# The opening of a fused transformer block: who splits and sums the input tiles, which queue loads the first two weight units, and who splits the memory units

## The chip, the cores and the metric

The kernel runs on one core of a Trainium2 chip. The metric is the device time of one execution in microseconds (us); a kernel's number is the median of its runs. The engines are TensorE (PE in the profile; PEld is its weight load), VectorE (DVE), ScalarE (ACT), GpSimd (POOL), and SyncE (SP), which issues most of the DMAs. ACT can issue DMAs too, on a queue of its own.

## The reference, cut to what matters

Two transformer blocks follow each other on 1024 tokens of width 1024, all in fp32. What the change touches is the head of the first:

```python
def rms_norm(x, w):
    y = x * lax.rsqrt(jnp.mean(x * x, axis=-1, keepdims=True) + 1e-6)
    return y * w

h = rms_norm(x, norm_w)                      # x: 1024 tokens x 1024
proj = einsum('bsd,de->bse', h, w_in)        # 1024 -> 6160: gq, gk, gv, glr, hq, ...
m = rms_norm(mem, mem_norm_w)                # mem: 256 tokens x 1024
mkv = einsum('bmd,de->bme', m, w_mem_kv)     # 1024 -> 1024: mk, mv
# two gated linear attentions, one cross attention over mk and mv, gate, w_out,
# then a convolution block and an MLP of width 4096 (the second block)
```

## The kernel before, in words

Activations lie transposed: x is eight tiles `xr[k]` (in RES) of 128 features by 1024 tokens. Weights come in "units" of 128 x 1024 fp32 (512 KB), listed in `UNITS` in the order of their use: unit 0 is `glr`, 1 `gq` of head 0, 2 `gk`, 3 and 4 `gv` of head 0, 5 to 8 the memory keys `mk`, 9 to 12 the memory values `mv`, 13 `gq` of head 1, and so on. There are four slots, so unit q is loaded when unit q - 4 has been read.

TensorE multiplies in a rounded fp32 form, so each operand is split into a high part (a rounded copy) and a low part (the rest), and a product is three matmuls: high weight with high data, high weight with low data, low weight with high data. A weight unit's high part goes to WH and its low part to WL. The low part is always a subtraction on GpSimd (L2480); the high part is a copy by ScalarE (through the helper at L1647) or by GpSimd (L2478), as the plan's `hi_by` says: ScalarE for units 0 and 1, GpSimd for those after them. Data goes to HB in the same way: the high part of an x tile (times `norm_w`) by ScalarE for even k and by GpSimd for odd k (L2463), the low part by VectorE (`stt` at L1963).

The norm's sum of squares: ScalarE squares each tile (L1666), and the squares are added into two accumulators, the even tiles on VectorE (`tt`, L1960), the odd ones on GpSimd (L2470). `x_sum` (L1261) then sums over the partitions with one-column matmuls against `ones`, VectorE scales it, GpSimd takes the power -1/2 (`root`, L2457), VectorE spreads it on a diagonal (p0dg), and `x_row` (L1268) makes a row of it in all partitions, which ScalarE copies to R. The projections run on x before that and are scaled by R afterwards.

`make_plan` writes one list of pieces, `P.order`; each engine's program walks it and emits its part of each piece. So the order on every engine is fixed when the program is built, and engines meet only at semaphores. VectorE and GpSimd each take their own instructions in turn. The order of the work on TensorE at the start is: `glr` and `gq` together, tile by tile (96 matmuls, L1250), `x_sum`, 30 matmuls of `gk`, `x_row`, the other 18 of `gk`, `m_sum` and the gate's matmuls (L1325), the four groups of 48 matmuls of `gv` (L1316), whose results ScalarE copies to VB, then `mk` (L1289) and `mv` (L1301). The group that is last of `gv` takes the PSUM bank of the first, so it waits for the first VB copies. ScalarE and VectorE split the memory tiles between them in `m_row` (mem to mhi and mlo), ahead of the VB copies in ScalarE's order.

Of the kernel before, what the change touches and what calls it, by code (L numbers as in the profile page):

```python
# [139 lines left out]
class Plan:  # L140
# [32 lines left out]
def make_plan():  # L173
# [10 lines left out]
    def u_split():  # L184
        q = split[0]
        while loaded[0] <= q:
            u_load()
        if not is_split(UNITS[q]):
            piece("split", q, hi_by[0])
        split[0] += 1  # L190
# [777 lines left out]
def build_program(nc, wall, wmod, xT, memT, vecs, gup, ident_d, masks_d, out, oscr, parts):  # L968
    es = ExitStack()
    with es:  # L970
# [80 lines left out]
        xsq = [at(f"p0sq{i}", 1024, F32, x0 + i * K4) for i in (1, 2, 4, 5)]  # L1051
        acc01 = [at("p0acc0", 1024, F32, x0 + 3 * K4), at("p0acc1", 1024, F32, x0 + 6 * K4)]
        dg0 = at("p0dg", 1024, F32, x0 + 4 * K4)
# [143 lines left out]
        def wait_x_done(w):  # L1197

            w.wait_ge(sig["x_lo"], 8)
            w.wait_ge(sig["x_add0"], 3)  # L1200
            w.wait_ge(sig["x_add1"], 3)


        def pe_program(pe):
# [24 lines left out]
            def wait_hb(gen, part, k, h):  # L1229
                if gen == 0:  # L1230
                    if part:
                        w.wait_ge(sig["x_lo"], k + 1)
                    else:
                        w.wait_ge(sig[f"x_hi{k % 2}"], k // 2 + 1)
                else:
                    kind = {1: ("m1_hi", "m1_lo"), 2: ("z_hi", "z_lo"), 3: ("m2_hi", "m2_lo")}[gen][part]
                    w.wait_ge(sig[kind], nth[kind, h, k])
# [16 lines left out]
            def x_sum():  # L1254
                bank, done = start(("x_sum",))
                w.wait_ge(sig["ones"], 1)
                w.wait_ge(sig["x_add0"], 3)
                w.wait_ge(sig["x_add1"], 3)
                for a in range(2):
                    for t in range(NT):  # L1260
                        i = pe.matmul(bank[:, t:t + 1], acc01[a][:, t * 128:(t + 1) * 128], ones[:, 0:1],  # L1261
                                      start=a == 0 and t == 0, stop=a == 1, skip_group_check=True)
                i.then_inc(done, 1)
# [379 lines left out]
        def act_program(ac):  # L1643
            w = Waits(ac)

            def copy(o, i, **kw):
                return ac.activation(o, i, ACT.Copy, **kw)  # L1647

            def x_hi_lo(k):
                if k % 2 == 0:  # L1650
                    w.wait_ge(sig[f"d_x{k}"], 16)
                    copy(hb(0, k), xr[k], scale=vcol("norm_w", k)).then_inc(sig["x_hi0"], 1)

# [7 lines left out]
            def x_square(k):  # L1661
                w.wait_ge(sig[f"d_x{k}"], 16)
                if k >= 6:
                    w.wait_ge(sig[f"x_add{k % 2}"], 1)
                o = acc01[k] if k < 2 else xsq[2 * (k % 2) + k // 2 % 2]
                ac.activation(o[:, :], xr[k], ACT.Square).then_inc(sig["x_sq"], 1)  # L1666

# [254 lines left out]
            def hid(i, h):  # L1922
# [17 lines left out]
                if i >= NH:  # L1940
# [6 lines left out]
                        x_turn=x_turn, x_value=x_value, silu_c=silu_c, mod_load=mod_load, mix=mix, sq_first=sq_first, sq=sq, m1_hi=m1_hi,  # L1947
                        m2_hi=m2_hi, glu=glu, pre=pre, ptap0=ptap0, ptap=ptap, ysq=ysq, z_hi=z_hi, hid=hid)
            w.wait_ge(sig["d_vec"], 16)
            w.wait_ge(sig["d_ident"], 16)  # L1950
# [5 lines left out]
        def dve_program(dv):  # L1956
# [17 lines left out]
            def x_hi_lo(k):  # L1974
                w.wait_ge(sig[f"x_hi{k % 2}"], k // 2 + 1)
                w.wait_ge(sig[f"d_x{k}"], 16)
                stt(hb(1, k), xr[k], vcol("norm_w", k), hb(0, k).bitcast(F32), ALU.mult, ALU.subtract).then_inc(sig["x_lo"], 1)

            def x_square(k):
                if k % 2 == 0 and k:  # L1980
                    w.wait_ge(sig["x_sq"], k + 1)
                    if k > 2:
                        w.wait_ge(sig["x_add0"], k // 2 - 1)
                    tt(acc01[0][:, :], acc01[0][:, :], xsq[k // 2 % 2][:, :], ALU.add).then_inc(sig["x_add0"], 1)

# [8 lines left out]
            def x_diag():  # L1994
                w.wait_ge(sig["x_pow"], 1)
                w.wait_ge(sig["x_add1"], 3)
                tt(*spread_of(dg0[:, :], xr_r, 8), ALU.mult).then_inc(sig["x_diag"], 1)
# [453 lines left out]
        def pool_program(po):  # L2451
# [6 lines left out]

            def x_hi_lo(k):
                if k % 2:  # L2460
                    w.wait_ge(sig[f"d_x{k}"], 16)
                    w.wait_ge(sig["d_vec"], 16)
                    po.tensor_scalar(hb(0, k), xr[k], vcol("norm_w", k), 0.0, ALU.mult, ALU.add).then_inc(sig["x_hi1"], 1)  # L2463

            def x_square(k):
                if k % 2 and k > 1:
                    w.wait_ge(sig["x_sq"], k + 1)
                    if k > 3:
                        w.wait_ge(sig["x_add1"], k // 2 - 1)
                    po.tensor_tensor(acc01[1][:, :], acc01[1][:, :], xsq[2 + k // 2 % 2][:, :], ALU.add).then_inc(sig["x_add1"], 1)  # L2470

            def split(q, by):
# [59 lines left out]
            def n4_sum(h):  # L2532
                wait_taken(w, "n4_sum", h)
                root(hs(R4, h), "n4_pow")

            work = dict(x_hi_lo=x_hi_lo, x_square=x_square, split=split, x_sum=x_sum, m_sum=m_sum, rms=rms, mix=mix,
                        n1_sum=n1_sum, pads=pads, ptap=ptap, ln_r=ln_r, n3_sum=n3_sum, n4_sum=n4_sum)
# [8 lines left out]
        def sp_program(sp):  # L2546
# [49 lines left out]

            work = dict(load=load, put_back=put_back, turn_o=turn_o, oi_load=oi_load, res_load=res_load, final=final)
            sp.dma_start(ident[:, :], ident_d).then_inc(sig["d_ident"], 16)
            sp.dma_start(vec[:, :], vecs).then_inc(sig["d_vec"], 16)
            load_x(0)  # L2600
            load(0)
            load_x(1)
            load_x(2)
            load(1)
            for k in range(3, 8):
                load_x(k)
            sp.dma_start(mraw[:, :], memT).then_inc(sig["d_mem"], 16)
            load(2)
            sp.dma_start(mst[:, :], masks_d).then_inc(sig["d_mask"], 16)
# [114 lines left out]
```

## Time and profile before

| | us |
|---|---|
| median of 3 runs | 2189.34 (2187.3 to 2192.83) |
| the profiled execution | 2192.47 |
| its span, first to last instruction | 2190.7 |
| TensorE busy | 2073.3 (95%) |
| TensorE's mean granted clock | 0.971 of full |

The profile gives for each engine when an instruction started and how long it took, what ended the idle time before it, and for stretches of time the busy share and the clock granted to TensorE (1.00 is 2.4 GHz, 0.50 is 1.2 GHz). A timeline row is: start, duration, engine, line, operation, result<-operands, shapes, count of merged instructions, and in brackets the idle time before it and who ended it. Matmul ends are modelled, so the distance between starts is the better measure of pace. TensorE's order is fixed, so what it loses at the start it does not win back later.

### The profile page before, as it was taken

The numbers are of one execution on the slowest core, as the hardware profiler recorded it, in microseconds if no ns is written. First come the engines' busy times: TensorE is split into PE (matmuls) and PEld (weight loads), VectorE is DVE, ScalarE is ACT, GpSimd is POOL, SyncE is SP. The second block draws the span as 40 slices with busy tenths as digits, with TensorE's granted clock in tenths as the row PEclk, the third lists the DMA queues.
The fourth block names the chain that finished last, engine by engine and source line by source line (L and its number), as shares of the span: only waits on it lengthen the run. The fifth ranks groups of instructions, "written<-read, shape, count | busy, mean of one in ns | idle before, by whom it ended". The sixth has DMA issues, their size and how long they took to land. (4 is left out here: it accounts for less than half of the span.)

```text
span 2190.7 us, 26491 instructions
## 1 busy us (share of the span) xinstructions
PE 2073.3 (95%) x10318; PEld 1729.1 (79%) x10318; DVE 1067.4 (49%) x1877; ACT 766.6 (35%) x1317; POOL 836.9 (38%) x497
## 2 busy tenths in 40 slices
PE   6899999999998789999989998799999999999997
PEld 5778989788887678888878786678787888888886
DVE  6354454456463244555559978996424112122125
ACT  2312322311126631221446656553425333312211
POOL 7252122212211243443428876673343444222220
PEclk9999999999899999999999999899899999999998
DMA  4121011101001296766434532123232333111112
GB/s 163 52 66 58 10 58 47 50 30 35 34 30 34 92 334 197 256 222 226 149 111 183 183 139 77 58 86 88 68 96 87 96 97 96 58 49 48 49 48 77
DMA packets 69420, 215.64 MB, mean 98 GB/s; under 512 B 7712, under 2 KB 8096, under 8 KB 69168
## 3 DMA queue, kind: packets, MB, share of 16 engines
q1 hardware_dynamic: 55472, 188.78, 25.6%
q10 hardware_dynamic: 13824, 25.17, 3.6%
q8 instruction: 82, 1.34, 0.3%
q14 instruction: 42, 0.34, 0.1%
HBM read 184.56 MB, written 29.36 MB: 98 GB/s over the span
## 5 line engine op out<-in xcount | busy, mean ns | idle before, releaser
L1250 PE MATMUL B<-HB,WH 128*128 128x512 f32 x2976 | 949.1, 405 | 26.2 <-ACT WH L1647 9.3
L2480 POOL TENSOR_TENSOR WL<-RAW,WH 128x1024 fp32r<-128x1024 f32 x205 | 497.5, 2429 | 592.3 <-ACT WH L1647 588.3
L1250 PEld LDWEIGHTS B<-HB,WH 128*128 128x128 f32 x2976 | 556.9, 192 | 148.2 <-issue 28.1
L1250 PE MATMUL B<-HB,WL 128*128 128x512 f32 x1488 | 574.7, 397 | 9.3 <-POOL WL L2480 9.3
L1250 PEld LDWEIGHTS B<-HB,WL 128*128 128x128 f32 x1488 | 284.8, 191 | 73.9 <-POOL WL L2480 12.7
L1647 ACT ACTIVATE WH<-RAW 128x1024 fp32r<-128x1024 f32 x164 | 173.0, 1056 | 451.7 <-DMA RAW<-wall 432.3
L1963 DVE SCALAR_TENSOR_TENSOR B<-UP,vec,B 128x512 f32<-128x512 f32 x308 | 207.3, 748 | 0.0
L1963 DVE SCALAR_TENSOR_TENSOR RES<-B,modv,RES 128x512 f32<-128x512 f32 x144 | 105.1, 747 | 208.6 <-PE B L1433 182.2
L1433 PE MATMUL B<-HIDH,WH 128*128 128x512 f32 x512 | 187.8, 400 | 4.5 <-DVE HIDL L1960 3.0
L2457 POOL TENSOR_TENSOR small<-small 128x4 f32<-128x4 f32 (+2 forms) x36 | 36.8, 1024 | 386.5 <-DVE small L1966 386.3
L1433 PE MATMUL B<-HIDH,WL 128*128 128x512 f32 x512 | 183.7, 392 | 0.0
L1433 PE MATMUL B<-HIDL,WH 128*128 128x512 f32 x512 | 183.6, 392 | 0.0
L1960 DVE TENSOR_TENSOR HIDL<-B,HIDH 128x512 fp32r<-128x512 f32 x64 | 44.1, 689 | 258.7 <-ACT HIDH L1647 258.7
L1316 PE MATMUL B<-WH,HB 128*128 128x256 f32 x768 | 148.8, 294 | 0.0
L2522 POOL TENSOR_TENSOR CO<-CO,PR 128x512 f32<-128x512 f32 x90 | 118.3, 1315 | 25.8 <-ACT PR L1893 13.3
L2478 POOL TENSOR_SCALAR WH<-RAW 128x1024 fp32r<-128x1024 f32 x41 | 46.9, 1145 | 211.6 <-DMA RAW<-wall 211.6
L1893 ACT ACTIVATE PR<-UP,vec 128x512 f32<-128x512 f32 x150 | 106.4, 724 | 57.8 <-POOL CO L2522 43.7
L1316 PEld LDWEIGHTS B<-WH,HB 128*128 128x128 f32 x768 | 123.1, 194 | 3.5 <-issue 1.5
L1433 PEld LDWEIGHTS B<-HIDH,WH 128*128 128x128 f32 x512 | 96.7, 189 | 27.4 <-DVE HIDL L1960 4.1
L1433 PEld LDWEIGHTS B<-HIDL,WH 128*128 128x128 f32 x512 | 96.7, 189 | 21.3 <-issue 1.9
L1433 PEld LDWEIGHTS B<-HIDH,WL 128*128 128x128 f32 x512 | 96.8, 189 | 20.4
L1316 PE MATMUL B<-WL,HB 128*128 128x256 f32 x384 | 109.6, 285 | 0.0
(242 smaller groups left out, 2689.1 us busy)
## 6 DMA issues: line engine op xcount, KB each, us to landing
RAW<-wall SPq DMA_DIRECT2D x205, 512.0 KB, 3.5
MODRAW<-wmod ACTq DMA_DIRECT2D x96, 256.0 KB, 4.4
WH<-parts SPq DMA_DIRECT2D x32, 512.0 KB, 3.2
WL<-parts SPq DMA_DIRECT2D x32, 512.0 KB, 4.2
RES<-xT SPq DMA_DIRECT2D x16, 512.0 KB, 8.9
oscr<-OT SPq DMA_DIRECT2D x32, 256.0 KB, 2.0
OI<-oscr SPq DMA_DIRECT2D x16, 512.0 KB, 5.2
parts<-WH SPq DMA_DIRECT2D x16, 512.0 KB, 5.2
```

The source lines that it names most:

```text
L1250: i = pe.matmul(bank, a[:, ks], hb(part, k, h), start=k == 0 and n == 0, stop=k == 7 and n == 2)
L1316: i = pe.matmul(bank[:, tl * 256:(tl + 1) * 256], hb(part, k)[:, t * 128:(t + 1) * 128], b[:, k % 4 * 256:(k % 4 + 1) * 256], start=k == 0 ...
L1433: i = pe.matmul(bank, a[:, ks], rhs(part, h), start=k == 0 and n == 0, stop=k == 3 and n == 2)
L1647: return ac.activation(o, i, ACT.Copy, **kw)
L1893: ac.activation(seg(buf[:, :]), tap(f, h, k), ACT.Copy, scale=wcol(f, k)).then_inc(sig["ptap_act"], 1)
L1960: return dv.tensor_tensor(o, a, b, op)
L1963: return dv.scalar_tensor_tensor(out=o, in0=a, scalar=s, in1=b, op0=op0, op1=op1)
L2457: po.tensor_tensor(o, o, mhalf[:, 0:n], ALU.pow).then_inc(sig[made], 1)
L2478: po.tensor_scalar(hi, raw, 1.0, 0.0, ALU.mult, ALU.add).then_inc(sig[f"w_hi{q % NW}"], 1)
L2480: po.tensor_tensor(lo, raw, hi.bitcast(F32), ALU.subtract).then_inc(sig[f"w_lo{q % NW}"], 1)
L2522: po.tensor_tensor(co, co, product_of[n][0][:, :], ALU.add).then_inc(sig["ptap"], 1)
```

## The change

Five edits, all in the first 125 us.

1. ScalarE makes all eight high parts of x, and makes them ahead of all squares. The high copy of unit 2 is on ScalarE too, between the two series.
2. VectorE alone adds the squares, seven additions into one accumulator; GpSimd has neither x tiles nor additions left. `x_sum` is 8 one-column products in place of 16.
3. Units 0 and 1 are loaded by ScalarE's own DMA queue; SyncE starts with tile 0 of x, then the vectors, the identity, and the other seven tiles.
4. ScalarE copies one element from `ones` to an unused column before it waits for any load, so that its function table is loaded then.
5. The high parts of the eight memory units (5 to 12) are made by ScalarE and no longer by GpSimd.

```diff
-            piece("split", q, hi_by[0])
+            piece("split", q, "act" if UNITS[q][0] in ("mk", "mv") else hi_by[0])
...
     for k in range(8):
         piece("x_hi_lo", k)
-        if k in (0, 2):
+        if k < 2:
             u_split()
+    u_split()
+    for k in range(8):
         piece("x_square", k)
...
             def x_sum():
                 bank, done = start(("x_sum",))
                 w.wait_ge(sig["ones"], 1)
-                w.wait_ge(sig["x_add0"], 3)
-                w.wait_ge(sig["x_add1"], 3)
-                for a in range(2):
-                    for t in range(NT):
-                        i = pe.matmul(bank[:, t:t + 1], acc01[a][:, t * 128:(t + 1) * 128], ones[:, 0:1],
-                                      start=a == 0 and t == 0, stop=a == 1, skip_group_check=True)
+                w.wait_ge(sig["x_add"], 7)
+                for t in range(NT):
+                    i = pe.matmul(bank[:, t:t + 1], xacc[:, t * 128:(t + 1) * 128], ones[:, 0:1], start=True, stop=True)
...
             def x_hi_lo(k):
-                if k % 2 == 0:
-                    w.wait_ge(sig[f"d_x{k}"], 16)
-                    copy(hb(0, k), xr[k], scale=vcol("norm_w", k)).then_inc(sig["x_hi0"], 1)
+                w.wait_ge(sig[f"d_x{k}"], 16)
+                copy(hb(0, k), xr[k], scale=vcol("norm_w", k)).then_inc(sig["x_hi"], 1)
...
             def x_square(k):
                 w.wait_ge(sig[f"d_x{k}"], 16)
-                if k >= 6:
-                    w.wait_ge(sig[f"x_add{k % 2}"], 1)
-                o = acc01[k] if k < 2 else xsq[2 * (k % 2) + k // 2 % 2]
-                ac.activation(o[:, :], xr[k], ACT.Square).then_inc(sig["x_sq"], 1)
+                if k > 4:
+                    w.wait_ge(sig["x_add"], k - 4)
+                ac.activation((xsq[(k - 1) % 4] if k else xacc)[:, :], xr[k], ACT.Square).then_inc(sig["x_sq"], 1)
...
+            for q in range(2):
+                ac.dma_start(RAW[:, slot(q)], wall[WALL.index(contents(UNITS[q])), :, :]).then_inc(sig[f"d_raw{q}"], 16)
+            w.wait_ge(sig["ones"], 1)
+            copy(small[:, 10:11], ones[:, 0:1])
...
             def x_square(k):
-                if k % 2 == 0 and k:
+                if k:
                     w.wait_ge(sig["x_sq"], k + 1)
-                    if k > 2:
-                        w.wait_ge(sig["x_add0"], k // 2 - 1)
-                    tt(acc01[0][:, :], acc01[0][:, :], xsq[k // 2 % 2][:, :], ALU.add).then_inc(sig["x_add0"], 1)
+                    if k > 1:
+                        w.wait_ge(sig["x_add"], k - 1)
+                    tt(xacc[:, :], xacc[:, :], xsq[(k - 1) % 4][:, :], ALU.add).then_inc(sig["x_add"], 1)
...
-            def x_hi_lo(k):
-                if k % 2:
-                    w.wait_ge(sig[f"d_x{k}"], 16)
-                    w.wait_ge(sig["d_vec"], 16)
-                    po.tensor_scalar(hb(0, k), xr[k], vcol("norm_w", k), 0.0, ALU.mult, ALU.add).then_inc(sig["x_hi1"], 1)
-
-            def x_square(k):
-                if k % 2 and k > 1:
...
-            sp.dma_start(ident[:, :], ident_d).then_inc(sig["d_ident"], 16)
-            sp.dma_start(vec[:, :], vecs).then_inc(sig["d_vec"], 16)
-            load_x(0)
-            load(0)
-            load_x(1)
-            load_x(2)
-            load(1)
-            for k in range(3, 8):
+            load_x(0)
+            sp.dma_start(vec[:, :], vecs).then_inc(sig["d_vec"], 16)
+            sp.dma_start(ident[:, :], ident_d).then_inc(sig["d_ident"], 16)
+            for k in range(1, 8):
                 load_x(k)
+            load(2)
             sp.dma_start(mraw[:, :], memT).then_inc(sig["d_mem"], 16)
-            load(2)
```

GpSimd's first instructions before (WL and WH are weight parts, HB the x parts, p0acc and p0sq the sums and squares):

```order
L2480 TENSOR_TENSOR WL<-RAW,WH 128x1024 [waits w_hi0,d_raw0,mhalf]
L2463 TENSOR_SCALAR HB<-RES,vec 128x1024 [waits d_vec,d_x1]
L2480 TENSOR_TENSOR WL<-RAW,WH 128x1024 [waits w_hi1,d_raw1]
L2463 TENSOR_SCALAR HB<-RES,vec 128x1024 [waits d_x3]
L2470 TENSOR_TENSOR p0acc_66<-p0acc_66,p0sq_64 128x1024 [waits x_sq]
L2463 TENSOR_SCALAR HB<-RES,vec 128x1024 [waits d_x5]
L2470 TENSOR_TENSOR p0acc_66<-p0acc_66,p0sq_63 128x1024 [waits x_add1,x_sq]
L2463 TENSOR_SCALAR HB<-RES,vec 128x1024 [waits d_x7]
L2470 TENSOR_TENSOR p0acc_66<-p0acc_66,p0sq_64 128x1024 [waits x_add1,x_sq]
L2478 TENSOR_SCALAR WH<-RAW 128x1024 [waits d_raw2]
L2480 TENSOR_TENSOR WL<-RAW,WH 128x1024 [waits w_hi2]
```

And GpSimd's first instructions after the change:

```order
L2466 TENSOR_TENSOR WL<-RAW,WH 128x1024 [waits w_hi0,d_raw0,mhalf]
L2466 TENSOR_TENSOR WL<-RAW,WH 128x1024 [waits w_hi1,d_raw1]
L2466 TENSOR_TENSOR WL<-RAW,WH 128x1024 [waits w_hi2,d_raw2]
L2464 TENSOR_SCALAR WH<-RAW 128x1024 [waits d_raw3]
L2466 TENSOR_TENSOR WL<-RAW,WH 128x1024 [waits w_hi3]
```

Four high parts, three additions and the high copy of unit 2 are gone from GpSimd ahead of unit 2's low part. VectorE before, from tile 6 of x to the mean of the squares:

```order
L1963 SCALAR_TENSOR_TENSOR HB<-RES,vec,HB 128x1024 [waits d_x6,x_hi0]
L1960 TENSOR_TENSOR p0acc_65<-p0acc_65,p0sq_62 128x1024 [waits x_add0,x_sq]
L1963 SCALAR_TENSOR_TENSOR HB<-RES,vec,HB 128x1024 [waits d_x7,x_hi1]
L1988 CAST masks<-mst 128x256 [waits d_mask]
L1988 CAST masks<-mst 128x256 x6
L1966 TENSOR_SCALAR small<-B 128x8 [waits full3]
```

And the same part of VectorE after the change:

```order
L1963 SCALAR_TENSOR_TENSOR HB<-RES,vec,HB 128x1024 [waits d_x6,x_hi]
L1963 SCALAR_TENSOR_TENSOR HB<-RES,vec,HB 128x1024 [waits d_x7,x_hi]
L1960 TENSOR_TENSOR p0acc<-p0acc,p0sq_61 128x1024 [waits x_sq]
L1960 TENSOR_TENSOR p0acc<-p0acc,p0sq_62 128x1024 [waits x_add,x_sq]
L1960 TENSOR_TENSOR p0acc<-p0acc,p0sq_63 128x1024 [waits x_add,x_sq]
L1960 TENSOR_TENSOR p0acc<-p0acc,p0sq_64 128x1024 [waits x_add,x_sq]
L1960 TENSOR_TENSOR p0acc<-p0acc,p0sq_61 128x1024 [waits x_add,x_sq]
L1960 TENSOR_TENSOR p0acc<-p0acc,p0sq_62 128x1024 [waits x_add,x_sq]
L1960 TENSOR_TENSOR p0acc<-p0acc,p0sq_63 128x1024 [waits x_add,x_sq]
L1988 CAST masks<-mst 128x256 [waits d_mask]
L1988 CAST masks<-mst 128x256 x6
L1966 TENSOR_SCALAR small<-B 128x8 [waits full3]
```

All seven additions now stand behind all eight low parts of x, and the seven mask casts stay behind them and ahead of the mean. ScalarE before, from the first head's last exponential (L1718) to its first VB copies (mhi is the memory tiles' high part, VB the values):

```order
L1718 ACTIVATE set0g<-set0g 128x1024 [waits taken0]
L1647 ACTIVATE mhi<-mem_71 128x256 [waits m_tm] x7
L1647 ACTIVATE mhi<-mem_71 128x256 [waits taken3]
L1647 ACTIVATE VB_78<-B,small 128x256 [waits full2]
L1647 ACTIVATE VB_78<-B,small 128x256
```

And the same place on ScalarE after the change (that exponential is L1714 here):

```order
L1714 ACTIVATE set0g<-set0g 128x1024 [waits taken0]
L1645 ACTIVATE WH<-RAW 128x1024 [waits full6,d_raw1]
L1645 ACTIVATE WH<-RAW 128x1024 [waits full5,d_raw2]
L1645 ACTIVATE mhi<-mem_70 128x256 [waits m_tm] x7
L1645 ACTIVATE mhi<-mem_70 128x256 [waits taken3]
L1645 ACTIVATE VB_77<-B,small 128x256 [waits full2]
L1645 ACTIVATE VB_77<-B,small 128x256
```

Two of the eight memory units' high copies come ahead of the memory tiles and the VB copies, the other six between the copies that follow.

## Rows read from the trace of the kernel before

**Rows 1.** The page's busy time, share of the span and instructions.

```profile
PE 2073.3 (95%) x10318; PEld 1729.1 (79%) x10318; DVE 1067.4 (49%) x1877; ACT 766.6 (35%) x1317; POOL 836.9 (38%) x497
```

**Rows 2.** Windows: length, each engine's busy us (instructions), PE clock, DMA, GB/s.

```profile
0.00:9.00 9.00, 0.00 (x0) 0.00 (x1) 0.80 (x1) 3.45 (x4) 0.45 (x6) 1.00 0.77 258
9.00:15.00 6.00, 4.23 (x8) 2.39 (x8) 2.64 (x3) 6.00 (x7) 5.75 (x3) 1.00 1.02 415
16.40:28.60 12.20, 12.20 (x53) 9.81 (x53) 11.25 (x6) 4.32 (x5) 12.20 (x5) 1.00 0.52 203
28.60:36.80 8.20, 6.15 (x25) 4.35 (x24) 8.20 (x4) 0.00 (x0) 8.12 (x4) 1.00 0.00 0
36.80:43.00 6.20, 3.95 (x10) 3.17 (x11) 6.20 (x7) 0.00 (x0) 5.59 (x3) 0.72 0.11 13
...
47.50:52.40 4.90, 4.90 (x13) 3.84 (x13) 2.22 (x2) 0.00 (x0) 4.34 (x3) 0.50 0.00 0
52.40:56.60 4.20, 4.20 (x19) 3.52 (x18) 0.00 (x0) 0.00 (x0) 1.58 (x1) 0.97 0.00 0
...
76.50:91.30 14.80, 14.80 (x123) 14.74 (x123) 8.12 (x18) 6.65 (x13) 0.00 (x0) 1.00 0.00 1
...
110.70:124.30 13.60, 12.09 (x51) 8.71 (x50) 0.00 (x0) 0.72 (x2) 13.27 (x9) 1.00 0.53 155
```

**Rows 3.** Waits in 0 to 60 us: total us, times, longest us.

```profile
PE B L1250 <- DVE HB L1963: 4.3, 3, 2.3
```

**Rows 4.** Timeline of ScalarE, 0 to 15 us.

```profile
5.54 1.28 ACT L1647 ACT_TABLE_LOAD   x1 [5.54 <-DMA RES<-xT]
6.83 1.15 ACT L1647 ACTIVATE HB<-RES,vec 128x1024 fp32r<-128x1024 f32 x1
...
12.71 1.99 ACT L1666 ACTIVATE p0sq<-RES 128x1024 f32<-128x1024 f32 x2
```

**Rows 5.** Timeline of VectorE and GpSimd, 12 to 45 us.

```profile
12.84 1.28 DVE L1963 SCALAR_TENSOR_TENSOR HB<-RES,vec,HB 128x1024 fp32r<-128x1024 f32 x1 [3.36 <-POOL HB L2463]
12.96 3.39 POOL L2480 TENSOR_TENSOR WL<-RAW,WH 128x1024 fp32r<-128x1024 f32 x1
...
23.87 3.36 POOL L2470 TENSOR_TENSOR p0acc<-p0acc,p0sq 128x1024 f32<-128x1024 f32 x1
24.90 3.41 DVE L1960 TENSOR_TENSOR p0acc<-p0acc,p0sq 128x1024 f32<-128x1024 f32 x1
...
38.92 4.51 DVE L1988 CAST masks<-mst 128x256 uint8<-128x256 f32 x7
```

**Rows 6.** DMA issues of the whole span: count, KB each, median us to landing.

```profile
RAW<-wall SPq DMA_DIRECT2D x205, 512.0 KB, 3.5
MODRAW<-wmod ACTq DMA_DIRECT2D x96, 256.0 KB, 4.4
```

**Rows 7.** Timeline from x_sum to x_row.

```profile
43.26 4.44 PE L1261 MATMUL B<-ones,p0acc 128*128 128x1 f32 x32
47.98 1.66 POOL L2457 TENSOR_TENSOR small<-small 128x8 f32<-128x8 f32 x1 [5.50 <-DVE small L1966]
49.68 2.06 DVE L1960 TENSOR_TENSOR p0dg<-ident,small 128x1024 f32<-128x1024 f32 x1 [1.78 <-POOL small L2457]
56.86 1.88 PE L1268 MATMUL B<-p0dg,ones 128*128 128x512 f32 x4
```

**Rows 8.** Timeline of ScalarE before and at the VB copies.

```profile
79.94 0.42 ACT L1647 ACTIVATE mhi<-mem 128x256 fp32r<-128x256 f32 x1 [0.47 <-DVE mem L1963]
90.24 2.28 ACT L1647 ACTIVATE VB<-B,small 128x256 f32<-128x256 f32 x6
```

**Rows 9.** Timeline of GpSimd and TensorE in the memory units.

```profile
101.03 1.05 POOL L2478 TENSOR_SCALAR WH<-RAW 128x1024 fp32r<-128x1024 f32 x1 [26.38 <-DMA RAW<-wall]
102.17 2.37 POOL L2480 TENSOR_TENSOR WL<-RAW,WH 128x1024 fp32r<-128x1024 f32 x1
104.59 0.39 PE L1289 MATMUL B<-mhi,WL 128*128 128x256 f32 x1 [1.22 <-POOL WL L2480]
```

More of the change, by code:

```diff
@@ L1051, in build_program @@
         xsq = [at(f"p0sq{i}", 1024, F32, x0 + i * K4) for i in (1, 2, 4, 5)]
-        acc01 = [at("p0acc0", 1024, F32, x0 + 3 * K4), at("p0acc1", 1024, F32, x0 + 6 * K4)]
+        xacc = at("p0acc", 1024, F32, x0 + 3 * K4)
         dg0 = at("p0dg", 1024, F32, x0 + 4 * K4)
@@ L1233, in wait_hb @@
                     else:
-                        w.wait_ge(sig[f"x_hi{k % 2}"], k // 2 + 1)
+                        w.wait_ge(sig["x_hi"], k + 1)
                 else:
@@ L1256, in x_sum @@
                 w.wait_ge(sig["ones"], 1)
-                w.wait_ge(sig["x_add0"], 3)
-                w.wait_ge(sig["x_add1"], 3)
-                for a in range(2):
-                    for t in range(NT):
-                        i = pe.matmul(bank[:, t:t + 1], acc01[a][:, t * 128:(t + 1) * 128], ones[:, 0:1],
-                                      start=a == 0 and t == 0, stop=a == 1, skip_group_check=True)
+                w.wait_ge(sig["x_add"], 7)
+                for t in range(NT):
+                    i = pe.matmul(bank[:, t:t + 1], xacc[:, t * 128:(t + 1) * 128], ones[:, 0:1], start=True, stop=True)
                 i.then_inc(done, 1)
@@ L1974, in x_hi_lo @@
             def x_hi_lo(k):
-                w.wait_ge(sig[f"x_hi{k % 2}"], k // 2 + 1)
+                w.wait_ge(sig["x_hi"], k + 1)
                 w.wait_ge(sig[f"d_x{k}"], 16)
@@ L1995, in x_diag @@
                 w.wait_ge(sig["x_pow"], 1)
-                w.wait_ge(sig["x_add1"], 3)
                 tt(*spread_of(dg0[:, :], xr_r, 8), ALU.mult).then_inc(sig["x_diag"], 1)
@@ L2457, in root @@
                 po.tensor_tensor(o, o, mhalf[:, 0:n], ALU.pow).then_inc(sig[made], 1)
-            def x_hi_lo(k):
-                if k % 2:
-                    w.wait_ge(sig[f"d_x{k}"], 16)
-                    w.wait_ge(sig["d_vec"], 16)
-                    po.tensor_scalar(hb(0, k), xr[k], vcol("norm_w", k), 0.0, ALU.mult, ALU.add).then_inc(sig["x_hi1"], 1)
-            def x_square(k):
-                if k % 2 and k > 1:
[L2467 to L2470, printed above, removed]
             def split(q, by):
@@ L2534, in n4_sum @@
                 root(hs(R4, h), "n4_pow")
-            work = dict(x_hi_lo=x_hi_lo, x_square=x_square, split=split, x_sum=x_sum, m_sum=m_sum, rms=rms, mix=mix,
+            work = dict(split=split, x_sum=x_sum, m_sum=m_sum, rms=rms, mix=mix,
                         n1_sum=n1_sum, pads=pads, ptap=ptap, ln_r=ln_r, n3_sum=n3_sum, n4_sum=n4_sum)
```

## The prediction, made before the changed kernel was run

> **What bounds the kernel now.** I read the page's busy shares first: TensorE is busy 95% of the span [rows 1], so all that the change can win is TensorE's time without work or at the low clock before about 125 us. Then the windows over that stretch [rows 2]. From 16.4 to 28.6 us TensorE issues a matmul every 0.23 us (12.20 / 53); in the next 8.2 us it is busy for 6.15; in the 6.2 us after those it is busy for 3.95, at a mean clock of 0.72. From 47.5 to 52.4 us the clock is 0.50, and 13 matmuls take 4.9 us. The table of waits names who was late: three waits of 4.3 us in all for the low x parts of VectorE, the longest 2.3 [rows 3]. Last come the timelines of the engines that make operands [rows 4, 5] and those of the memory units [rows 9], where TensorE waits for GpSimd's low parts.
>
> The timeline of VectorE and GpSimd shows why VectorE is late [rows 5]. Its two-input operation takes 1.28 us alone (12.84), and GpSimd's takes 2.37 alone (102.17, [rows 9]). Where both have work, each takes about the sum: 3.39 for the GpSimd one that starts 0.12 us behind VectorE's, 3.36 for the next, 3.41 for the VectorE addition that starts while it runs. They take turns and do not overlap. So what counts in this stretch is the sum over both engines: some 1.2 us per VectorE operation, 2.3 per GpSimd subtraction or addition, 1.05 per GpSimd copy (101.03, [rows 9]).
>
> **The first stage, to x_sum.** Before, GpSimd has 13 operations until the two splits after x are done: 7 of 2.3 and 6 of 1.05, 22.4 us. After, it has 4 low parts and one copy: 10.3 us. VectorE goes from 8 low parts and 3 additions (13.2 us) to 8 and 7 (18.0). The sum falls from 35.6 to 28.3 us, and what TensorE waits for (the low parts of x) now stands ahead of all additions.
>
> When does it start? ScalarE's first copy came at 6.83, after a wait to 5.54 for the load and a table load of 1.28 [rows 4]. The table load moves ahead of the data, so it costs nothing there. The load itself lies between 4.5 us (the 0.27 MB of vectors and identity no longer ahead of x, at the 258 GB/s of the first 9 us [rows 2]) and 7.5 (0.8 MB of the other queue in between, 1.9 us at 415 GB/s). I take 6.9, near the upper end, since the first copy needs the vectors and the identity too: no gain. Tiles then land every 1.26 us (0.52 MB at 415 GB/s), tile 1 at about 9.2, and ScalarE's copies of 1.0 to 1.15 us [rows 4] keep up: tile 1 at 10.4, unit 1 at 11.4, tile 7 at 18.2, unit 2 at 19.4, squares from there at 1.0 each.
>
> The Trainium skill, "DMA: Bandwidth & Descriptors", section "Issuing engines are not separate DMA queues", speaks against this edit: DMAs of different issuing engines run on the same 16 DMA engines and interleave, so a second queue only saves issue time. By it the start would be at the 7.5 end; if the queues did not disturb each other, at the 4.5 end. What decides below is tile 1, so neither moves the sum by more than 1 us. The skill's "ScalarE: Activation LUTs", section "What ACT_TABLE_LOAD costs", gives 1.28 us and a drain of 1.38 behind it; the row has the copy 0.01 us behind the table load, so here only 1.28 can be won.
>
> Now in turns: unit 0's low part until 11.6, x tile 1's to 12.8, unit 1's to 15.1. That is TensorE's last early obstacle: it has issued 8 matmuls by then, as before, when unit 1's low part came at 16.35 (12.96 + 3.39, [rows 5]). The other 88 at 0.23 are 20.0 us: to 35.1, or 35.7 if the clock rises a little late. VectorE goes on: tiles 2 to 5 by 19.9, unit 2's low part 22.2, tile 6 23.4, unit 3's copy 24.5, tile 7 25.7, unit 3's low part 28.0, seven additions 36.4. TensorE reaches tile 6 at about 31, so no x part is late any more; the last addition and the last matmul come together, and x_sum starts at 36.0 to 36.4 in place of 43.26 [rows 7]. Bounds: 34.5 (nothing in the way) and 43 (as now).
>
> **From x_sum to x_row.** x_sum was 32 issued matmuls in 4.44 us [rows 7], partly at half clock; half of them at full clock are 1.5 us. Behind it stand 30 matmuls: 9.16 us from 47.70 to 56.86, since the clock was 0.50 for 4.9 us; at full clock they take 6.9. That makes 8.4 us. The other chain is as long: behind the last addition the masks (4.51, [rows 5]), then mean, power (1.66) and diagonal (2.06) [rows 7], 8.6 us with the hand-offs. The masks now stand in the way of the mean: the wait that the change adds. So x_row starts at 36.2 + 8.6 = 44.8 if the clock holds: **12.1 us won**. If it falls as before, x_sum takes up to 2.9 and the matmuls 9.16, and x_row comes at 48.3: 8.6 won. I take the first, since a stretch with 2 us idle (28.6 to 36.8) kept 1.00 [rows 2], while the low stretches followed an idle time of 2.3 us [rows 3] and 4.44 us of one-column matmuls; 1.5 us of them is nearer to the first.
>
> **From x_row to the values.** The other 18 matmuls, the memory's squares, m_sum and the gate are the same chain as before, so the gain is carried. Then two copies of 1.0 us stand ahead of the memory tiles on ScalarE. It was idle 0.47 us there before 79.94 [rows 8], so the chain of memory tiles and VB copies behind it comes 1.5 us later. The first two VB copies ended about 91.1 (90.24, with six in 2.28), and TensorE's last group of values began at 97.1 - 48 x 0.12 = 91.3 (pace of 14.80 / 123, [rows 2]): 0.2 us of slack. So **1.2 us lost**; at least nothing, at most 1.9, or more if the clock is higher there than now, but then TensorE only waits for what it had run ahead.
>
> **The memory units.** GpSimd's pace before is 3.5 us a unit (copy 1.05, low part 2.37, [rows 9]); TensorE needs 24 x 0.12 = 2.9 for an `mk` and 12 x 0.23 = 2.7 for an `mv`. From 97.1 to 124.3 its eight units took 27.2 us where 22.4 would do. With the copies on ScalarE, GpSimd's pace is 2.4. The first unit loaded in this stretch lands at 101.03 as before, its copy and low part still come one behind the other, so the wait of 1.2 us at 104.59 [rows 9] stays. Behind it: `mk` 2 to 107.3, `mk` 3 to 110.2, four `mv` to 121.1. The slack is thin but there: unit 12 is free to load at 110.2, lands 3.5 later [rows 6], has copy and low part by 117.1, and is needed at 118.3. **3.2 us won**, and 0.5 behind it, since GpSimd, which worked 13.27 of 13.60 us here [rows 2], is no longer late for the next head's first unit. The new copies also hold back MK and MV copies queued behind them on ScalarE by up to 2 us; a bank is asked for again two units (5.6 us) later, so TensorE does not feel it. Bounds: 0 and 4.8.
>
> **The sum.** -12.1 + 1.2 - 3.2 - 0.5 = -14.6 us. The profiled execution took 2192.47 (span 2190.7 and 1.8 around it), so it would take 2177.9. That execution is 3.1 above the median of 2189.34, and against the median the forecast is **2174.7 us**. Nothing behind 125 us changes, and TensorE's order there is fixed.
>
> **Rivals.**
> - The clock falls behind x_sum anyway (or rises late at the start). For it: it fell there before, and TensorE may stand idle a moment for the last addition. Against it: half as many skinny matmuls and no stall shortly before. 8.6 in place of 12.1: 2178.2. Chance 0.22.
> - The second queue delays the start. Unit 0 or the vectors land 3 us later than I take, and as ScalarE's order is fixed, everything behind moves with them. For it: on ScalarE's queue 256 KB took 4.4 us to land, where 512 KB on SyncE's took 3.5 [rows 6]. Against it: those were measured beside other transfers, and here the issue is the first of the program. 2177.7. Chance 0.12.
> - VectorE becomes the bound and the kernel slower. If each of its 15 operations took the 3.41 us of the contended row, they would last to 8.2 + 51.2 = 59.4, x_row would start at 68.0, and the whole would be 11.1 later less 2.5: 2198. It decides from where the 15 average 2.8 us (x_row 2.5 us late). Against it: GpSimd has 10.3 us of work in place of 22.4 in that time, and only with it does VectorE take turns. Chance 0.05.
> - It does what it says and most of it is hidden: the first stage bound by loads, the memory part by the order on ScalarE (unit 12 behind the fourth MK copy). Half of the first term and none of the memory's: 6 - 1.2, about 2184.5. Chance 0.09.
> - The forecast itself: 0.52, with 2171 to 2178 as its own range.
>
> The range reaches from 2168 (first stage at 34.5, the full 4.8 in the memory units) to 2184, which leaves out the slow case and most of the hidden one. What a measurement can tell from no change is 0.3%, 6.6 us: from 2182.8 down it is faster. Faster: the forecast, the first two rivals and a part of the fourth, 0.87. Same 0.08, slower 0.05.
>
> **What would show it.** No wait of TensorE for VectorE's x parts after 16 us, and no GpSimd operation above 2.4 us unless VectorE works beside it. First x_sum matmul at 35 to 37, x_row at 44 to 46. ScalarE's first copy with no table load ahead of it. A new wait of 1 to 2 us of TensorE for a VB copy before the last group of values. In `mk` and `mv` one wait of 1.2 us left, and `mv` done 27.2 - 3.2 = 24.0 us after `mk` starts. It is wrong if x_sum starts after 40, if the additions take over 2 us each with GpSimd idle, or if unit 0 lands after tile 1.

## The result, and the profile after

The change is faster, by much less than forecast: 2186.9 us median against 2192.4 for the kernel before (20 runs each), a ratio of 0.9976 with a 95% interval of 0.9968 to 0.9985. That is 5.3 us won (3.3 to 7.0), where 14.6 were forecast, and it is less than the 0.3% that the prediction took as the least that can be told from no change; with 20 runs of each the interval leaves no change out. The ratio and its interval compare fast executions with fast ones. The profiled execution took 2183.27 us (span 2181.5).

The page's busy line, against [rows 1]:

```profile
PE 2070.9 (95%) x10302; PEld 1728.6 (79%) x10302; DVE 1066.4 (49%) x1881; ACT 779.2 (36%) x1331; POOL 808.2 (37%) x481
```

GpSimd has 16 instructions fewer, ScalarE 14 more, TensorE 16 fewer. Where the time went is read from TensorE's waits in the first 60 us (total us, times, longest) and from 60 to 130 us:

```profile
PE B L1251 <- ACT WH L1645: 10.6, 1, 10.6
PE B L1251 <- POOL WL L2466: 1.8, 2, 1.4
PE B L1260 <- DVE p0acc L1960: 1.0, 1, 1.0
PE B L1272 <- DVE mem L1960: 3.2, 1, 3.2
...
PE B L1314 <- ACT VB L1645: 3.1, 1, 3.1
PE B L1287 <- POOL WL L2466: 1.3, 1, 1.3
```

The wait for VectorE's x parts [rows 3] is gone; in its place stands one of 1.0 us for the last addition. But the first wait, for the first weight unit, has grown (to 10.6 us from 9.0, counted from the span's start), and there is a new one of 3.1 us for the VB copies. The 3.2 us at L1272, for the memory's squares, stand in the kernel before too. The timelines of ScalarE (0 to 15 us), TensorE and VectorE, against [rows 4, 7]:

```profile
1.66 1.28 ACT L1645 ACT_TABLE_LOAD   x1 [1.66 <-PEq L2697]
2.95 0.20 ACT L1645 ACTIVATE small<-ones 128x1 f32<-128x1 f32 x1
8.39 1.15 ACT L1645 ACTIVATE HB<-RES,vec 128x1024 fp32r<-128x1024 f32 x1 [5.24 <-DMA ident<-ident]
...
37.98 1.92 PE L1260 MATMUL B<-ones,p0acc 128*128 128x1 f32 x16 [1.02 <-DVE p0acc L1960]
48.29 1.88 PE L1266 MATMUL B<-p0dg,ones 128*128 128x512 f32 x4
...
9.76 1.28 DVE L1963 SCALAR_TENSOR_TENSOR HB<-RES,vec,HB 128x1024 fp32r<-128x1024 f32 x1 [9.76 <-ACT HB L1645]
28.65 9.19 DVE L1960 TENSOR_TENSOR p0acc<-p0acc,p0sq 128x1024 f32<-128x1024 f32 x7
```

The table load is out of the way, yet the first copy of x starts at 8.39 and not at 6.83: it waited 5.24 us for the identity. x_sum comes at 37.98 (43.26 before), x_row at 48.29 (56.86 before), 8.6 us earlier. Next ScalarE, VectorE and GpSimd from the gate to the VB copies, against [rows 8]:

```profile
70.80 1.99 ACT L1645 ACTIVATE WH<-RAW 128x1024 fp32r<-128x1024 f32 x2
72.69 0.40 ACT L1645 ACTIVATE mhi<-mem 128x256 fp32r<-128x256 f32 x1
85.23 2.28 ACT L1645 ACTIVATE VB<-B,small 128x256 f32<-128x256 f32 x6
...
72.01 4.94 POOL L2466 TENSOR_TENSOR WL<-RAW,WH 128x1024 fp32r<-128x1024 f32 x2 [12.87 <-ACT WH L1645]
...
73.13 1.56 DVE L1960 TENSOR_TENSOR mlo<-mem,mhi 128x256 fp32r<-128x256 f32 x1 [1.78 <-ACT mhi L1645]
75.69 1.54 DVE L1960 TENSOR_TENSOR mlo<-mem,mhi 128x256 fp32r<-128x256 f32 x1 [0.48 <-ACT mhi L1645]
78.23 0.43 DVE L1960 TENSOR_TENSOR mlo<-mem,mhi 128x256 fp32r<-128x256 f32 x1 [0.48 <-ACT mhi L1645]
```

The copies of units 5 and 6 stand ahead of the memory tiles, and their low parts on GpSimd, which before were done 5 us before this chain began, now run beside it: two of VectorE's eight subtractions take 1.55 us in place of 0.43. The VB copies start 36.9 us behind x_row; before it was 90.24 - 56.86 = 33.4. Windows of TensorE around the last group of values (length, busy us and counts of PE, PEld, DVE, ACT, POOL, clock, DMA, GB/s):

```profile
82.90:86.10 3.20, 0.15 (x2) 0.00 (x0) 1.84 (x5) 1.61 (x5) 0.00 (x0) 0.84 0.00 0
86.10:92.30 6.20, 6.20 (x30) 6.20 (x31) 0.00 (x0) 1.41 (x4) 0.00 (x0) 0.53 0.01 3
92.30:94.50 2.20, 2.20 (x21) 2.20 (x19) 0.00 (x0) 0.00 (x0) 0.00 (x0) 1.00 0.00 0
```

TensorE stands for 3.1 us and then works about 6 us at 1.2 GHz. Of the 8.6 us won at x_row, 2.7 are left at the last VB copy (94.70, 97.41 before). The memory units then give back what was forecast: the MV copies come at 117.99 in place of 123.97, 23.3 us behind the last VB copy in place of 26.6.

### The profile page after: what moved, and what is told of

It is laid out like the page before. It is cut to its first block and busy times, and to the rows that moved or that the text cites. A ratio compares the mean times of both kernels' runs of the same rounds, so it can differ in the third digit from the quotient of the medians.

```text
span 2181.5 us, 26463 instructions
## 1 busy us (share of the span) xinstructions
PE 2070.9 (95%) x10302; PEld 1728.6 (79%) x10302; DVE 1066.4 (49%) x1881; ACT 779.2 (36%) x1331; POOL 808.2 (37%) x481
## 5 line engine op out<-in xcount | busy, mean ns | idle before, releaser
L1251 PE MATMUL B<-HB,WH 128*128 128x512 f32 x2976 | 948.9, 405 | 22.8 <-ACT WH L1645 10.6
L1645 ACT ACTIVATE WH<-RAW 128x1024 fp32r<-128x1024 f32 x173 | 182.4, 1056 | 455.0 <-DMA RAW<-wall 440.4
L2464 POOL TENSOR_SCALAR WH<-RAW 128x1024 fp32r<-128x1024 f32 x32 | 35.7, 1116 | 188.6 <-DMA RAW<-wall 188.6
```

The source lines that it names most:

```text
L1251: i = pe.matmul(bank, a[:, ks], hb(part, k, h), start=k == 0 and n == 0, stop=k == 7 and n == 2)
L2464: po.tensor_scalar(hi, raw, 1.0, 0.0, ALU.mult, ALU.add).then_inc(sig[f"w_hi{q % NW}"], 1)
```

## The experiments

Theory A was that the copies of units 5 and 6 cost more, in that place, than all eight units bring: by the queue on ScalarE, by the turns of VectorE and GpSimd, and by the clock behind the wait. Theory L was that the second queue holds the start back. Ratios are to the kernel before, on the same chip; a mark is the start of the MV copies. Where no ratio is given the variant ran once, and only its trace is read. A low stretch is time in which the granted clock is 1.2 GHz. How far the mark lies behind x_row leaves the luck of the first 50 us out: in the four profiles of the kernel before it is 67.1 to 67.4 us, in the two of the changed kernel 69.7 and 69.0.

**mem_back**: the changed kernel without its memory edit.

```diff
-            piece("split", q, "act" if UNITS[q][0] in ("mk", "mv") else hi_by[0])
+            piece("split", q, hi_by[0])
```

> The changed kernel with the memory units' high parts back on GpSimd; everything else as changed. Theory A (the two copies ahead of the memory tiles on ScalarE, and the two GpSimd low parts that they push beside VectorE's part of the same chain, hold back the VB copies; TensorE waits 3.1 us for them and then runs the next 6.8 us at 1.2 GHz): no wait for VB, no low clock there, mv done about 8.6 us earlier than in the kernel before less nothing won in the memory units, so MV copies at 115.4; against before -9 us, ratio 0.996. Rival B (the loss between x_row and the values is the clock's own, whatever stands on ScalarE): the last group of values still runs partly at 1.2 GHz and the ratio is that of the changed kernel or worse, 0.998 to 1.000.

Measured: ratio 0.9964 (0.9952 to 0.9976), no wait for VB, no low clock there, x_row at 48.48 and VB copies 33.4 us behind it, mark 116.02. The mark is 67.5 us behind x_row, as in the kernel before. Without the memory edit the kernel is no worse than with it, by these ratios rather better (the intervals touch). Theory A's sizes hold; the rival falls.

**mem_from_7**: units 5 and 6 split by GpSimd, 7 to 12 by ScalarE.

```diff
-            piece("split", q, "act" if UNITS[q][0] in ("mk", "mv") else hi_by[0])
+            piece("split", q, "act" if UNITS[q][0] in ("mk", "mv") and q > 6 else hi_by[0])
```

> The changed kernel with units 5 and 6 split by GpSimd as before and units 7 to 12 by ScalarE. Theory A: both gains together, 8.6 at the start and 3.3 + 0.5 in the memory units: MV copies at 112, against before -12.4 us, ratio 0.9943. Rival B: as the changed kernel, -5 to -6, ratio 0.9976. A third way, that the ScalarE copies of units 7 to 12 hold back MK copies and so TensorE: a wait of TensorE in mk or mv beyond the one of 1.3 us.

Measured: 0.9934 (0.9919 to 0.9949), mark 110.93. Its ScalarE at the VB and MV copies:

```profile
80.53 2.28 ACT L1645 ACTIVATE VB<-B,small 128x256 f32<-128x256 f32 x6
87.70 0.84 ACT L1645 ACTIVATE VB<-B,small 128x256 f32<-128x256 f32 x2 [4.89 <-PE B L1314]
110.93 1.28 ACT L1645 ACTIVATE MV<-B 128x512 f32<-128x512 f32 x2 [5.65 <-PE B L1299]
```

Taking two of the eight units back brings 7 us at the mark. Some 1.4 of them are not its doing: x_row came at 46.89, without a low stretch ahead of it. Behind x_row the mark comes after 64.0 us, so the edit itself is worth 4.9 to 5.7. TensorE's only wait in the memory units is the one of 1.2 us that was forecast to stay.

**two_idle_copies**: mem_back, and two copies of the raw memory tiles to an unused place where those of units 5 and 6 stood.

```diff
-            piece("split", q, "act" if UNITS[q][0] in ("mk", "mv") else hi_by[0])
+            piece("split", q, hi_by[0])
...
+        SPARE = at("SPARE", 1024, F32, o + 6 * K4)
...
+                if q in (5, 6):
+                    if q == 6:
+                        w.wait_ge(sig["spare"], 1)
+                    ac.activation(SPARE[:, :], mraw[:, 0:1024], ACT.Copy).then_inc(sig["spare"], 1)
```

> mem_back with two extra ScalarE copies of 128 x 1024 (from the raw memory tiles to an unused place) where the changed kernel has its copies of units 5 and 6. They delay ScalarE as those do, but GpSimd's low parts stay early. It parts theory A's two causes. If queueing alone does it, the VB copies come 1.5 us late and TensorE waits 1.2 to 1.4; if the two engines' taking turns adds 2 us, as in the changed kernel (mlo rows of 1.56 and 1.54 in place of 0.42), it is absent here and the wait stays below 1.6, where the changed kernel has 3.1. Rival: 3.1 here too, then the GpSimd side plays no part.

Measured: the VB copies start 81.87 - 47.15 = 34.7 us behind x_row, where mem_back has 33.4. TensorE's wait for them, and VectorE's first subtractions:

```profile
PE B L1315 <- ACT VB L1646: 0.7, 1, 0.7
...
72.01 0.42 DVE L1965 TENSOR_TENSOR mlo<-mem,mhi 128x256 fp32r<-128x256 f32 x1 [1.66 <-ACT mhi L1646]
73.44 0.43 DVE L1965 TENSOR_TENSOR mlo<-mem,mhi 128x256 fp32r<-128x256 f32 x1 [0.48 <-ACT mhi L1646]
```

So the queue on ScalarE is worth 1.3 us, and the rest of the delay of 3.6 in the changed kernel is the turns: twice 1.1 us, as its two long rows say. No low clock followed the wait of 0.7.

**before_mem_only**: the kernel before with the memory edit alone.

```diff
-            piece("split", q, hi_by[0])
+            piece("split", q, "act" if UNITS[q][0] in ("mk", "mv") else hi_by[0])
```

> The kernel before with only the memory units' high parts on ScalarE. Theory A: the wait for VB costs 3 to 3.4 us and a low stretch behind it up to 3 more, the memory units give 3.8 back: -0.5 to +2.5 us against before, ratio 1.000. Rival (this edit was a gain of 3 us as forecast, and the start gave less than its x_row shows): -2.5 us, ratio 0.9988.

Measured: 1.0011 (0.9999 to 1.0023), a wait for VB of 3.7 us, a low stretch of 3.4 us behind it, and 23.3 us from the last VB copy to the mark. The mark is 68.9 us behind x_row. The edit that was forecast to bring 2.5 us brings nothing by itself, and costs some 1.7 up to the mark.

**one_queue**: mem_from_7 with the loads of the kernel before.

```diff
-            for q in range(2):
-                ac.dma_start(RAW[:, slot(q)], wall[WALL.index(contents(UNITS[q])), :, :]).then_inc(sig[f"d_raw{q}"], 16)
...
+            sp.dma_start(ident[:, :], ident_d).then_inc(sig["d_ident"], 16)
+            sp.dma_start(vec[:, :], vecs).then_inc(sig["d_vec"], 16)
             load_x(0)
-            sp.dma_start(vec[:, :], vecs).then_inc(sig["d_vec"], 16)
-            sp.dma_start(ident[:, :], ident_d).then_inc(sig["d_ident"], 16)
-            for k in range(1, 8):
+            load(0)
+            load_x(1)
+            load_x(2)
+            load(1)
+            for k in range(3, 8):
                 load_x(k)
+            sp.dma_start(mraw[:, :], memT).then_inc(sig["d_mem"], 16)
             load(2)
-            sp.dma_start(mraw[:, :], memT).then_inc(sig["d_mem"], 16)
```

> mem_from_7 with the loads as in the kernel before: one queue, identity and vectors first, unit 0 behind tile 0, unit 1 behind tile 2. Theory L (the second queue delays the start: ScalarE's first copy waited until 8.39 us for the identity, behind 1 MB of unit 0 and 1 that the other queue moved at the same time): the first copy at 5.6, with no table load ahead of it, TensorE starts at 7.8 in place of 10.6, unit 1's low part comes at about 15, x_sum starts at 36.4 in place of 38.2; against before -14, ratio 0.9936, one to two us better than mem_from_7. Rival (the engines' taking turns sets x_sum, whatever lands first): first copy at 5.6, but x_sum at 37.5 to 38.2 and no difference in the whole.

Measured: 0.9935 (0.9916 to 0.9955). ScalarE, 5 to 40 us:

```profile
5.79 1.15 ACT L1645 ACTIVATE HB<-RES,vec 128x1024 fp32r<-128x1024 f32 x1 [3.55 <-DMA RES<-xT]
7.83 1.06 ACT L1645 ACTIVATE WH<-RAW 128x1024 fp32r<-128x1024 f32 x1 [0.89 <-DMA RAW<-wall]
...
11.62 1.06 ACT L1645 ACTIVATE WH<-RAW 128x1024 fp32r<-128x1024 f32 x1 [1.39 <-DMA RAW<-wall]
...
21.90 1.06 ACT L1645 ACTIVATE WH<-RAW 128x1024 fp32r<-128x1024 f32 x1 [2.75 <-DMA RAW<-wall]
```

The first copy comes 2.8 us sooner than in mem_from_7, which has two queues, as theory L said, but x_sum only 0.8 sooner, at 37.39: this order of loads lets ScalarE wait for units 1 and 2. The whole shows no difference to mem_from_7. Both expectations were half right.

**two_queues_vec_first**: both queues, SyncE with the vectors and the identity ahead of tile 0.

```diff
-            load_x(0)
             sp.dma_start(vec[:, :], vecs).then_inc(sig["d_vec"], 16)
             sp.dma_start(ident[:, :], ident_d).then_inc(sig["d_ident"], 16)
-            for k in range(1, 8):
+            for k in range(8):
```

> mem_from_7 with both queues, but SyncE issues vectors and identity ahead of tile 0. If the order on SyncE alone made the first copy late, it comes at 6.5 or sooner; if it is the bytes of the other queue that land between, tile 0 is now the last to land and the copy still starts at 7.8 to 8.4. x_sum within 1 us of 38.2 either way.

Measured: first copy at 8.09, now released by tile 0, and x_sum at 37.68. The order on SyncE's queue moves the first copy by 0.3 to 0.8 us against the six profiles with tile 0 first (8.39 to 8.88). What the other queue costs is read against best_from_7 below, where SyncE issues the same three loads in the same order and there is no second queue:

```profile
8.09 1.15 ACT L1645 ACTIVATE HB<-RES,vec 128x1024 fp32r<-128x1024 f32 x1 [4.94 <-DMA RES<-xT]
```

```profile
6.93 1.15 ACT L1645 ACTIVATE HB<-RES,vec 128x1024 fp32r<-128x1024 f32 x1 [4.70 <-DMA RES<-xT]
```

So the bytes of the other queue cost some 1.1 us at the first copy (7.04 in best_early). The Trainium skill, "DMA: Bandwidth & Descriptors", section "Issuing engines are not separate DMA queues", has this rule, that DMAs of different issuing engines interleave on the same 16 DMA engines, and these rows agree. The rest of the 2.8 us of one_queue lies in the order on its one queue: with the identity ahead of the vectors it had the first copy at 5.79, with the vectors first it came 1.1 to 1.3 later. Why that order matters no run shows.

**no_table_ahead**: mem_from_7 without the one-element copy.

```diff
-            w.wait_ge(sig["ones"], 1)
-            copy(small[:, 10:11], ones[:, 0:1])
```

> mem_from_7 without the one-element copy, so that the table load stands behind the wait for tile 0, vectors and identity. First x copy at 9.7 in place of 8.4. If the start of the x copies sets the stage, x_sum comes 1.3 us later, at 39.5; if tile 1 and the turns do, 38.2 to 38.7. The page's drain of 1.38 us behind a table load is not there: the copy starts within 0.05 us of the load's end.

Measured, ScalarE and TensorE:

```profile
8.35 1.28 ACT L1645 ACT_TABLE_LOAD   x1 [8.35 <-DMA ident<-ident]
9.65 1.15 ACT L1645 ACTIVATE HB<-RES,vec 128x1024 fp32r<-128x1024 f32 x1
...
39.23 1.92 PE L1260 MATMUL B<-ones,p0acc 128*128 128x1 f32 x16
```

The first copy is 1.07 us later than in mem_from_7 (8.58), and x_sum 1.05 later (38.18). So the start of the x copies moves x_sum one for one, as long as ScalarE does not wait for a later load as in one_queue; the forecast had said that it would move the sum by 1 us at most over its whole range. Between the table load's end and the copy there are 0.02 us; no drain shows.

**mem_early**: the changed kernel with ScalarE's copies of units 5 and 6 ahead of the gate.

```diff
+    while loaded[0] < 7:
+        u_load()
+    u_split()
+    u_split()
     for h in range(2):
         piece("glr", h)
```

> The changed kernel with ScalarE's copies of units 5 and 6 moved ahead of the gate's pieces, where ScalarE waited 4.4 us for TensorE. All eight memory units are then on ScalarE, and neither the queue ahead of the memory tiles nor the turns beside them is left. Theory A: as mem_from_7, no wait for VB, MV copies at 111 to 112.5, ratio 0.9934. Rival: unit 6 lands too late (it is loaded when gk is done, 54.3 us, and lands 3.5 us later), the gate's first copy at 61.2 moves by up to 1 us, ratio 0.994.

Measured: 0.9950 (0.9929 to 0.9970), no wait for VB, VB copies 33.4 us behind x_row, mark 110.79. The same eight units on the same engine as in the changed kernel, with the copies of units 5 and 6 at 55.40 in a place where ScalarE had been idle, and 6.6 to 7.2 us are back at the mark. Again some 1.4 of them lie ahead of x_row (46.91); behind it the mark comes after 63.9 us, 5.1 to 5.8 sooner than in the changed kernel. It is the place that cost, not the work.

**best_early** and **best_from_7**: mem_early and mem_from_7 with one queue in the order of use.

```diff
-            for q in range(2):
-                ac.dma_start(RAW[:, slot(q)], wall[WALL.index(contents(UNITS[q])), :, :]).then_inc(sig[f"d_raw{q}"], 16)
...
-            load_x(0)
             sp.dma_start(vec[:, :], vecs).then_inc(sig["d_vec"], 16)
             sp.dma_start(ident[:, :], ident_d).then_inc(sig["d_ident"], 16)
-            for k in range(1, 8):
+            load_x(0)
+            load(0)
+            load_x(1)
+            load(1)
+            for k in range(2, 8):
                 load_x(k)
```

> mem_early with one queue in the order of use: vectors, identity, tile 0, unit 0, tile 1, unit 1, tiles 2 to 7, unit 2, raw memory. one_queue had ScalarE's first copy at 5.79 but waited for unit 1 until 11.62 and for unit 2 until 21.90. Theory L: first copy at 5.8, unit 1's copy at 9.9, unit 2's at 19, x_sum at 36 (38.2 less the 2.6 by which the chain starts earlier, plus up to 0.5 of waits for tiles), MV copies at 109; against before -15, ratio 0.9930. Rival (the tiles' landing every 1.26 us sets the chain's pace, so an early start is lost by tile 7): x_sum at 37.4 as in one_queue.

> The same loads with mem_from_7's split (units 5 and 6 by GpSimd). x_sum and MV copies as in best_early to 0.5 us; the ratio the same within its interval, 0.9930.

Measured: 0.9945 (0.9927 to 0.9963) and 0.9936 (0.9913 to 0.9959). The first copy came at 7.04 and 6.93, not at 5.8 as expected, x_sum at 36.43 and 36.39, the mark at 108.68 and 110.58. x_sum is 1.8 us sooner than with two queues, so theory L holds for that step, and its rival, that the tiles' landing sets the pace, falls; in the whole kernel it doesn't show, since the intervals are as wide as the gain. The two marks differ by the low stretch behind x_sum, which best_from_7 had and best_early had not. The four variants that free the VB copies (these two, mem_from_7, mem_early) and one_queue cannot be told from each other, but each beats the kernel before, and all but mem_early also lie clear of the changed kernel's first interval. All seven variants without the wait for VB and with ScalarE's copies (these five and the two that ran once, two_queues_vec_first and no_table_ahead) have the mark 63.6 to 64.1 us behind x_row.

**after_again**: the changed kernel, unedited, once more.

> The changed kernel once more. Theory A: the wait for VB is 3.1 us again and a low stretch follows it, of 3.4 or 6.8 us. The low stretch behind x_sum (40.1 to 43.9 in the first profile, absent in mem_from_7, whose program is the same up to there) is chance: present or not, x_row at 48.3 or at 46.9. Rival: it is there each time.

Measured: 0.9978 (0.9963 to 0.9994). The wait for VB is 3.5 us, the low stretch behind it 3.4 us where it had been 6.8, and the stretch behind x_sum is there again. x_row is at 48.43. Over the six profiles whose program is the same up to x_row (after, after_again, mem_back, mem_from_7, two_idle_copies, mem_early) it stood three times at 48.3 to 48.5 with that stretch and three times at 46.9 to 47.2 without it, mean 47.7. It is not there each time, as expected, but it is not shown to be chance alone: in the three with it TensorE had just waited 0.9 to 1.1 us for the last addition, in the three without it 0 to 0.2. The other five variants fit that less well: best_from_7 (0.7 us) and one_queue (0.2) had it, best_early (0.5) and the two that did not wait had it not.

**before_a, before_b, before_c**: the kernel before, unedited, because before_mem_only had its x_row at 53.90.

> The kernel before, unchanged, to see where its x_row lies. Theory C (the clock's low stretches ahead of x_row are chance): x_row between 53.5 and 57, x_sum at 41.9 or at 43.3 depending on whether the stall behind x tile 6 drops the clock. Rival (they follow from the stalls each time): x_sum at 43.3 and x_row at 56.9 to 0.3 us.

> The kernel before a second time: by theory C x_row anywhere between 53.5 and 57 us, by the rival at 56.9 to 0.3 us.

> The kernel before a third time: by theory C x_row anywhere between 53.5 and 57 us, by the rival at 56.9 to 0.3 us.

Measured: their x_row rows in that order, first the one of before_mem_only:

```profile
53.90 1.88 PE L1268 MATMUL B<-p0dg,ones 128*128 128x512 f32 x4
```

```profile
55.47 1.88 PE L1268 MATMUL B<-p0dg,ones 128*128 128x512 f32 x4
```

```profile
56.84 1.88 PE L1268 MATMUL B<-p0dg,ones 128*128 128x512 f32 x4
```

```profile
58.78 1.88 PE L1268 MATMUL B<-p0dg,ones 128*128 128x512 f32 x4
```

With the 56.86 of the profile shown the mean of five is 56.4. The rival, 56.9 each time, falls, and the last of them lies beyond theory C's 57 too. The same instructions differ by 5 us, but the profile from which I forecast was only 0.5 above the mean: the starting point explains 0.5 us of the miss, and not the 3 that the 53.90 had seemed to say.

## Why the prediction was wrong, point by point

Up to the mark the forecast was -12.1 + 1.2 - 3.2 = -14.1 us. The mean mark of the kernel before is 124.2 (four profiles), that of the changed kernel 117.7 (two): -6.5, near the 5.3 of the medians. The first two points below make 3.4 us of the difference of 7.6, the third 3.9 to 4.7. The 0.5 us forecast behind the mark is there: the wait of 0.5 for the next head's first low part is gone.

- **The first stage, to x_sum: mechanism right, start mis-sized.** The forecast had the first x copy at 6.9, bounds 4.5 to 7.5; it came at 8.4 to 8.9, outside them. The forecast counted 0.8 MB of the other queue ahead of it, but the copy stands behind all of three loads (0.79 MB), and both units (1.05 MB) shared the DMA engines with them; the two queues against the best order on one queue cost 2.8 us, of which some 1.1 are shown to be the other queue's bytes. And "what decides below is tile 1" was wrong: after the first copy nobody waits for a load, and VectorE works on with one gap of 0.5 us, so the 1.5 to 2.0 us went straight to x_sum: 38.2 in the mean of six against 36.2. The turns themselves were right: 28.2 us were forecast from VectorE's first low part to the end of the last addition (8.2 to 36.4), and 28.1 were measured (9.76 to 37.84).
- **x_sum to x_row: the rival with the low clock, half of the time.** 8.6 us were forecast and came in the executions without a low stretch (46.89 - 38.18 = 8.7); with it 10.3. The forecast gave it 0.22; it came in three of six. Together with the 0.5 of the starting point: 8.7 us won (56.4 - 47.7) in place of 12.1.
- **The failed step: "1.2 us lost" at the VB copies.** It was to be 1.5 us of delay less 0.2 of slack. The delay is 3.6 (3.8 in after_again, 3.9 in before_mem_only): the queue costs 1.3 (two_idle_copies), the turns of VectorE and GpSimd 2.2. The forecast had used the rule of the turns for the first stage and not here, though the change moves GpSimd's low parts as well as ScalarE's copies: a low part waits for its high part. And the wait has a tail: the clock stood at 1.2 GHz for 3.4 us behind it, or for 6.8 us from its last third on, 1.2 and 2.3 us more from the first VB copy to the last (8.4 and 9.5 us against 7.2). So 5.1 to 5.9 us were lost, where "at most 1.9" was the bound. The forecast had no term for a low clock behind this wait.
- **The memory units: right.** 26.6 us from the last VB copy to the MV copies became 23.3, 3.3 won against 3.2, with one wait of 1.3 left.
- **The masks** were said to stand in the way of the mean. They took 1.50 us in place of 4.51 [rows 5], since GpSimd no longer works beside them; TensorE's x_sum was later than they were.
- **The range.** Its lower end does not follow from the two terms named for it: a first stage at 34.5 in place of 36.2 and 4.8 in place of 3.2 give 2171.4, not 2168. A smaller slip: 88 matmuls at 0.23 us are 20.2 us, not 20.0.

## What to carry to other kernels

When an operation moves to another engine, move its consumers too in the reckoning: here two copies went to ScalarE, and it was the subtractions behind them on GpSimd that fell on VectorE's critical chain. Put such work where its new engine is idle (ScalarE had 4.4 us without work in front of the gate) and not just ahead of a chain that TensorE waits for. A wait of TensorE of 3 us in otherwise dense work is to be priced with the half clock around its end (here each of 3.1 to 3.7 us had one), and a load's landing by all bytes in flight on all queues until the last thing that the first instruction needs.

## What the runs showed of the hardware

Three things that the forecast did not reckon with. VectorE's mask casts (one input, fp32 to uint8) take turns with GpSimd too: seven in 4.51 us with GpSimd's subtraction beside part of them [rows 5], seven in 1.50 us alone, as in after_again:

```profile
37.89 1.50 DVE L1988 CAST masks<-mst 128x256 uint8<-128x256 f32 x7
```

In the kernel before the median cast took 0.28 us; one that started at 38.9 took 1.13 and ended with GpSimd's copy (37.89 to 39.90), and one from 40.2 took 2.46 and ended with its subtraction (39.99 to 42.48). The Trainium skill, "SBUF — State Buffer", section "Who interferes with whom", names casts in their two-port modes among what contends with GpSimd. These rows agree, though none shows in which mode the casts ran.

The clock's low stretches differ from one execution to the next, and what places them is not shown: in five executions of the same instructions TensorE reached x_row between 53.90 and 58.78 us, with low stretches of 3.4 to 13.8 us ahead of it. A gain of 2 us at the start of this kernel cannot be read from one profile.

And one low stretch was there in all sixteen profiles, before and after: TensorE waits 3.2 us for the memory's squares (the row at L1272 above), and the clock is at 1.2 GHz for some 10.3 us, beginning within 1 us of that wait's end (66.2 to 76.6 us in the kernel before, 57.6 to 68.2 in the changed one). The change leaves it alone. An estimate from the VB tail (2.3 us lost in 5.8 us of work at 1.2 GHz) makes the low stretch worth some 4 us on top of the wait, more than the memory units' term.
